# Row weights by small transfers instead of 4-row products, with a reordered first stage and router

## The chip, the cores and the metric

The kernel runs on one core of a Trainium2 chip. The metric is the device time of one execution in microseconds (us), lower is better. Times of the profile are those of one profiled execution; engines are named as the profile names them: PE (matrix multiplies, PEld its weight loads), DVE (VectorE), ACT (ScalarE), POOL (GpSimd), SP (SyncE, which only issues DMAs).

## What is computed

One inference step of a one-layer encoder trunk on 336 tokens: 64 of a sample stream, 16 learned meta tokens and 256 prompt tokens, model width 1024, all float32. The parts that matter here, cut from the reference:

```
z = rmsnorm(x, g_mix) @ w_in            # first stage, then the projections
qk = silu(causal_conv(qk_pre)); ig, lf = gates of 4 heads from z
# mLSTM, per chunk of 64 tokens (one of 16), 4 heads
inter = b + m;  m_t = max(inter, max(d))
w_intra = exp(d - m_t);  w_inter = exp(inter - m_t)
s = (q @ k.T) * w_intra
num = s @ v + w_inter * (q @ C)
h = num / max(|qn|, exp(-m_t));  C_new = w_prev * C + (w_k * k).T @ v
# latent attention beside it: o_v ("ov"), both merged by gates and w_out
x = x + mixed @ w_out
x2 = rmsnorm(x, g_ffn)
logits = x2 @ w_router + b_router       # top 4 of 32 experts, softmax gates
x = x + sum over the 4 of gate * (swiglu(x2 @ w_gu[e] + b_gu[e]) @ w_dn[e] + b_dn[e])
y = rmsnorm(x, g_final)
```

`w_inter` is one number per head and token. In the kernel a head's weights are a row of 336 numbers on one partition, while the queries that they scale lie with their features on 128 partitions, so each row must reach all partitions. The same holds for the running maximum, which enters `w_intra`.

## The kernel before

Tokens are handled as three row tiles of 128, 128 and 80 (`ROWS`) where they lie on partitions, and as six chunks (`CHUNKS`) in attention and recurrence. The order of the work on each engine is written out by hand, and `job_list` gives the order in which the eight PSUM banks are used: job n uses bank n mod 8, `begin` waits until the job eight places before has been read out (`take`), `filled` waits for PE's result.

**First stage.** SP issues the loads of x, then the identity matrix, then the weight panels in the order of need. ACT issues eight loads of small vectors (`vec_rows`, `conv_rows`), takes the three sums of squares, then three roots; DVE scales the three tiles (L1446), PE turns them ("xT"), DVE multiplies by the norm's gain on the way out of PSUM (L1436), and the first projection `("cq", 0)` begins. The gates of the recurrence (`igfr`) come next; DVE works them out in rows of 4 partitions after a wait on `ld_mem`, which counts the broadcast of the router's bias too. Then come the low-rank keys (`lat`), which `keys_turned` needs.

**Attention.** Four pairs of heads (`hp`), each with nine steps `c` in which scores, softmax and value products of six chunks are staggered. Between these steps whole projections are put in as cover (`mla_fill`: query/key and value columns, eight 128x336 products each). In the last pair, the steps 5 and 6 have such a cover, and step 7 has the four products "wi".

**Recurrence's row weights.** `wrow` holds two rows for each of 4 heads: `R_MX` (running maximum) and `R_WI` (w_inter). "wi" are four products of a selector of 4 rows x 128 with `R_WI`, one for each head; ACT copies them to `wib` and takes `wprev` (the weight at the end of each chunk) from there. "mx" are four such products onto 64 partitions each with `R_MX` (L807); DVE turns them into `emat` with the causal mask. After these come the turn of `tail` ("convrow"), the last attention value products `values_out(3)` ("ov"), a wait until ACT has copied these, and the keys and values of chunk 0 turned onto tokens (`keys_values_turned(0)`), then the projection `("o", 0)`.

**Router and experts.** For each row tile: output products ("out", two halves of 512 columns), residual (DVE), norm (ACT square and root, DVE `x2`), turn ("x2T"), router ("lg"), top 4 (DVE `choose`). PE counts with `chosen` which expert gets which token; DVE builds the tables (`tab`, `be`), also the gates as a matrix of tokens by experts (`gmat`), which PE turns ("gT"). POOL gathers the first 64 token rows from DRAM (`rows_in`), PE turns them, ACT copies them to `xg`, and the loop over blocks of 64 tokens starts (`gate_up` at L1030 and L1036, `down` at L1056). SP streams the weights of an expert (12 MB) in 12 transfers, each issued when PE has consumed the piece that it overwrites. `keep_going` issues 128x512 products whose result nobody reads.

## Time and profile before

| what | us |
|---|---|
| median of 3 runs | 1691.27 (1687.09 to 1694.07) |
| the profiled execution | 1689.88 |
| its span, first to last instruction | 1688.1 |
| PE busy in the span | 1530.1 |
| DVE busy in the span | 355.5 |
| ACT busy in the span | 349.8 |
| POOL busy in the span | 122.3 |

The stages by the trace: first stage up to 19.16 us (the first projection starts), projections and attention to about 300 us, recurrence, gates and merging to 532 us, output, router and tables to 605.56 us (the first product of an expert), experts and the final norm to the end.
### The profile page before, as it was taken

To read this page: it belongs to the slowest core of one execution; us is meant where nothing else is said; L and a number is where in the kernel's file an instruction comes from. 1 tells how busy PE (TensorE), PEld (TensorE's weight loads), DVE (VectorE), ACT (ScalarE), POOL (GpSimd) and SP (SyncE) were. 2 spreads that over 40 slices of the span, in tenths; PEclk is the share of its full clock that TensorE was granted. 3 is DMA by queue.
4 is the path that set the end of the run, shared out by engine and by line. 5 is a ranking of instruction groups with operands and counts; after the bars stand their busy time and mean duration, and the time that the engine had idled before them with its cause. 6 is when DMAs were issued, how large, how long until landed. Compare 5 with 4: busy or idle time off the path is not lost.

```text
span 1688.1 us, 20518 instructions
## 1 busy us (share of the span) xinstructions
PE 1530.1 (91%) x7108; PEld 698.8 (41%) x7109; DVE 355.5 (21%) x859; ACT 349.8 (21%) x676; POOL 122.3 (7%) x219
## 2 busy tenths in 40 slices
PE   6999999999999999788799988878999887998993
PEld 4666666666665533222233332222333222333331
DVE  3655432243301330101010110100111001011015
ACT  3434423543200201111111110111111111111111
POOL 0100000000000000001001010000010000001010
PEclk9999999999999989899899998989999998999997
DMA  6311222212284359999989899999898999669897
GB/s 234 107 57 71 101 99 76 76 51 100 90 282 165 133 191 401 408 419 417 408 325 408 341 415 416 416 406 422 321 405 355 410 414 405 262 266 414 342 411 271
DMA packets 92393, 477.38 MB, mean 283 GB/s; under 512 B 12995, under 2 KB 16944, under 8 KB 43074
## 3 DMA queue, kind: packets, MB, share of 16 engines
q1 hardware_dynamic: 84312, 461.79, 69.1%
q0 software_dynamic: 7808, 15.00, 2.7%
q8 instruction: 23, 0.38, 0.1%
q10 hardware_dynamic: 234, 0.08, 0.0%
q14 instruction: 16, 0.13, 0.0%
HBM read 471.28 MB, written 15.50 MB: 288 GB/s over the span
## 4 chain that ended last, share of the span: by engine, by line
PE 73%; DMA 18%; DVE 4%; issue 3%; SPq 1%; ACT 1%; DVEq 0%; POOL 0%; ACTq 0%; POOLq 0%
PE bank L611 28%; PE bank L1030 21%; DMA ring<-in_w_gate_up 17%; PE bank L1056 16%; PE bank L615 3%; PE bank L1036 1%; DVE r_kv L1436 1%; DVE r_v L1439 1%; PE bank L878 1%; DVE r_c L1439 1%; DVE r_qk L1433 0%; SPq L565 0%; PE bank L724 0%; SPq L572 0%; PE bank L873 0%
## 5 line engine op out<-in xcount | busy, mean ns | idle before, releaser
L1030 PE MATMUL bank<-ring,r_kv 128*64 128x512 f32 x2184 | 521.1, 624 | 87.1 <-DMA ring<-in_w_gate_up 87.1
L1030 PEld LDWEIGHTS bank<-ring,r_kv 128*64 128x64 f32 x2184 | 157.1, 142 | 398.5 <-issue 305.6
L1056 PE MATMUL bank<-ring,r_kv 128*64 128x512 f32 x1248 | 289.5, 607 | 0.7 <-ACT r_kv L1126 0.7
L611 PE MATMUL bank<-r_xt,ring 128*128 128x336 f32 x848 | 250.9, 451 | 2.6 <-DVE r_xt L1436 2.4
L1433 DVE TENSOR_SCALAR r_kv<-bank 128x512 f32<-128x512 f32 (+1 forms) x80 | 55.0, 687 | 921.6 <-PE bank L1036 916.1
L611 PEld LDWEIGHTS bank<-r_xt,ring 128*128 128x128 f32 x848 | 159.1, 191 | 79.8 <-issue 8.0
L1056 PEld LDWEIGHTS bank<-ring,r_kv 128*64 128x64 f32 x1248 | 92.6, 143 | 196.0 <-issue 195.1
L1126 ACT ACTIVATE r_xt<-bank 128x512 f32<-128x512 f32 x39 | 23.3, 598 | 507.0 <-PE bank L1056 507.0
L1379 ACT ACTIVATE r_o<-r_kv 128x512 f32<-128x512 f32 x39 | 24.6, 632 | 323.7 <-DVE r_kv L1433 323.7
L615 PEld LDWEIGHTS bank<-const,r_v 64*128 64x128 f32 (+3 forms) x524 | 49.7, 157 | 77.5 <-DVE r_v L1439 44.0
L1036 PE MATMUL bank<-ring,r_kv 128*64 128x512 f32 x312 | 73.5, 592 | 0.0
L615 PE MATMUL bank<-const,r_v 64*128 64x64 f32 (+3 forms) x524 | 64.0, 258 | 10.4 <-DVE r_v L1439 10.4
L611 PE MATMUL bank<-ring 128*128 128x336 f32 (+2 forms) x288 | 70.6, 434 | 0.0
L1126 ACT ACTIVATE r_kv<-bank 128x512 f32<-128x512 f32 (+3 forms) x85 | 49.8, 586 | 82.2 <-PE bank L615 76.9
L611 PE MATMUL bank<-ring,r_kv 128*128 128x128 f32 (+4 forms) x192 | 59.1, 444 | 1.2 <-DVE r_kv L1436 1.2
L611 PEld LDWEIGHTS bank<-ring 128*128 128x128 f32 (+2 forms) x288 | 45.9, 192 | 21.4 <-issue 3.9
L1379 ACT ACT_TABLE_LOAD x39 | 50.0, 1283 | 12.8 <-ACT r_xt L1126 12.6
L1020 PE MATMUL bank<-bgu,r_qk 32*64 32x512 f32 x312 | 43.3, 624 | 8.8 <-DVE r_kv L1433 8.8
L1949 POOL COPY r_qk<-r_qk 128x1 uint32 x39 | 7.9, 202 | 554.8 <-ACT r_xt L1126 554.8
L1953 POOL DMA_INDIRECT y_rows<-r_xt,r_qk x39 | 41.1, 1053 | 34.4 <-POOL r_qk L1949 34.4
L1925 POOL DMA_INDIRECT r_v<-x_rows,r_qk x41 | 39.4, 961 | 54.6 <-POOL r_qk L1942 33.1
L611 PEld LDWEIGHTS bank<-ring,r_kv 128*128 128x128 f32 (+3 forms) x192 | 30.3, 182 | 28.8 <-issue 23.2
(248 smaller groups left out, 945.8 us busy)
## 6 DMA issues: line engine op xcount, KB each, us to landing
ring<-in_w_gate_up SPq DMA_DIRECT2D x256, 1024.0 KB, 17.8
ring<-in_w_down SPq DMA_DIRECT2D x128, 1024.0 KB, 14.9
ring<-in_w_in SPq DMA_DIRECT2D x12, 2048.0 KB, 8.2
ring<-in_w_proj_b SPq DMA_DIRECT2D x2, 2048.0 KB, 8.4
ring<-in_w_proj_a SPq DMA_DIRECT2D x2, 2048.0 KB, 9.3
ring<-in_w_out SPq DMA_DIRECT2D x2, 2048.0 KB, 7.9
ring<-y_rows SPq DMA_DIRECT2D x8, 512.0 KB, 8.5
ring<-in_w_uq SPq DMA_DIRECT2D x2, 1152.0 KB, 8.9
```

Source lines behind the costliest of these rows:

```text
L611: ins = pe.matmul(out, l, r, start=(n == 0), stop=(n == len(pairs) - 1), **kw)
L615: return pe.transpose(out, src, ident[0:src.shape[0], 0:src.shape[0]])
L1020: pe.matmul(half(gate_bank if q < 2 else up_bank, q % 2), pick[32 * q:32 * q + 32, :], bgu[32 * q:32 * q + 32, :], start=True, stop=False, ...
L1030: ins = pe.matmul(half(gate_bank if q < 2 else up_bank, q % 2), xg[:, k, :], w[:, 512 * q:512 * q + 512], start=False, stop=False, skip_gr ...
L1036: ins = pe.matmul(half(bank_, t), xg[:, 7, :], w[:, 512 * (q0 + t):512 * (q0 + t) + 512], start=False, stop=True, skip_group_check=True)
L1056: ins = pe.matmul(half(out_bank, t), hidT[:, 2 * (j % 2) + s, BLK * h:BLK * h + BLK], w[:, s, 512 * t:512 * t + 512], start=(j == 0 and s ...
L1126: return act.activation(out, src, ACT.Copy, scale=scale)
L1379: act.activation(sg, gt, ACT.Sigmoid, scale=ALPHA).then_inc(m_sig, 1)
L1433: return dve.tensor_scalar(out, a, s1, s2, op0, op1)
L1439: return dve.scalar_tensor_tensor(out=out, in0=a, scalar=s, in1=b, op0=op0, op1=op1)
L1925: pool.indirect_dma_start(xrow, None, x_rows_dram[:, :], bass.IndirectOffsetOnAxis(ap=column[0:BLK, :].bitcast(U32), axis=0), bounds_check ...
L1953: pool.indirect_dma_start(y_rows_dram[:, :], bass.IndirectOffsetOnAxis(ap=now[:, 1:2].bitcast(U32), axis=0), yrow, None, bounds_check=8 * ...
```

## The change

It has three parts, and a fourth that follows from them.

1. **First stage.** The identity is loaded by ACT's queue ahead of everything else; one more small vector (the gain of the second norm) is loaded. ACT does a root on a dummy value first, and then square and root of tile 0 before the squares of tiles 1 and 2. DVE scales each tile as soon as its root is there, and the way out of PSUM is shared: ACT does the second half of tiles 0 and 1 (eight copies of 128x128), DVE the other four. PE issues 20, 4, 4 and 7 products of 128x128 whose result nobody reads (`warm`) around the turns. ACT squares both `ckv` before it does the gates' exponentials.
2. **Row weights.** POOL writes `wrow` to DRAM (into rows of `y_rows`) when the gates are done, waits for that, and loads it back broadcast: the maxima onto twice 64 partitions (`emat`), the weights of heads 2 and 3 onto 128 (`wib_hi`), and later, when the convolutions no longer use `u_pad`, those of heads 0 and 1 into `u_pad`. POOL takes `wprev` from there; DVE applies the mask at the start of the second pair of heads. The eight products, ACT's twelve copies and the selector are gone. In the last pair of heads, the projections that stood in steps 5 and 6 stand in 6 and 7. `values_out(3)` stands behind `keys_values_turned(0)`.
3. **Router.** PE turns the residual x1 half by half as soon as it is there, rather than the normed x2; the norm's gain is multiplied into the router's weights, and its scale is applied to the logits. x2 is still made for the gather.
4. **Gates.** The normalised gates, `gmat` and its turn move behind the tables and into the first expert's products; the bias products of the first block move ahead of the turn of the gathered rows.

The core of the diff:

```diff
 def mla_fill(hp, at):
 
+    if hp == 3:
+        at = {5: None, 6: 5, 7: 6}.get(at, at)
     n = 6 * hp + FILL_AT[at] if at in FILL_AT else len(FILL_MLA)
...
+            def warm(b, n):
+
+                for _ in range(n):
+                    pe.matmul(b[:, 0:128], ident, ident, start=True, stop=True, skip_group_check=True)
+
             pe.wait_ge(ld_ident, 16)
...
+            warm(begin("convT"), 20)
             for t, (c0, n) in enumerate(ROWS):
+                if t == 1:
+                    pe.wait_ge(ld_vec, 128)
+                    b = begin("vecT")
+                    end(turn(b[:, 0:NVEC], vec_rows[0:NVEC, :]), "vecT")
+                    warm(begin("convT"), 4)
+                if t == 2:
+                    warm(begin("convT"), 4)
                 pe.wait_ge(xn_ready, t + 1)
...
+            pe.wait_ge(ld_conv, 16)
+            b = begin("convT")
+            end(turn(b[:, 0:48], conv_rows[:, :]), "convT")
+            warm(begin("cq", 0), 7)
...
-                    if hp == 3 and c == 7:
-                        for h in range(4):
-                            b = begin("wi", h)
-                            end(group(b[:, 0:NT], [(cst("sel", 4)[:, 128 * h:128 * h + 128], R_WI)]), "wi", h)
-            for p in range(2):
-                b = begin("mx", p)
-                for g in range(2):
-                    h = p + 2 * g
-                    ins = pe.matmul(b[64 * g:64 * g + 64, 0:NT], cst("sel", 4)[:, 128 * h:128 * h + 64], R_MX, start=True,
-                                    stop=True, skip_group_check=True)
-                end(ins, "mx", p)
...
-            values_out(3)
...
             keys_values_turned(0)
+            values_out(3)
+            for hp in range(4):
+                for h in (0, 1):
+                    taken(pe, "ov", hp, h)
...
             out_half(0, 0)
             out_half(0, 1)
...
+            out_half(1, 0)
+            x1_turned(0, 0)
+            x1_turned(0, 1)
+            out_half(1, 1)
+            pe.wait_ge(w_rt_set, 1)
+            router(0)
+            out_half(2, 0)
+            x1_turned(1, 0)
+            x1_turned(1, 1)
+            out_half(2, 1)
+            x1_turned(2, 0)
+            router(1)
+            x1_turned(2, 1)
...
             count(0)
-            keep_going(begin("x2T", 2, 0), 2)
-            x2_turned(2)
             router(2)
...
+            def gates_turned():
+
+                pe.wait_ge(gates_set, 1)
+                for t, (c0, m) in enumerate(ROWS):
+                    ins = turn(xt_bank[0:NE, c0:c0 + m], gmat[0:m, t, :])
+                ins.then_inc(gT_full, 1)
+
             pe.wait_ge(ld_bgu, 64)
             bias(0)
+            nb = pe.value_load(nbi[0:1, 0:1].bitcast(I32), min_val=NE, max_val=MAXB)
+            pe.wait_ge(m_xrow, 16)
+            tokens_turned()
             pe.wait_ge(m_xg, 1)
             for k in range(8):
+                if k == 1:
+                    gates_turned()
...
+            pool.wait_ge(gates4, 1)
+            pool.dma_start(y_rows_dram[0:8, 0:NT].rearrange("(q h) t -> h q t", q=2), wrow[:, :, :]).then_inc(gates_out, 16)
+            pool.wait_ge(gates_out, 16)
+            for g in range(2):
+                pool.dma_start(emat[64 * g:64 * g + 64, :, :],
+                               y_rows_dram[2 * g:2 * g + 2, 0:NT].unsqueeze(0).broadcast_to([64, 2, NT])).then_inc(mx_in, 16)
+            pool.dma_start(wib_hi[:, :, :], y_rows_dram[6:8, 0:NT].unsqueeze(0).broadcast_to([128, 2, NT])).then_inc(wi_in, 16)
...
+            pool.wait_ge(tail_done, 16)
+            pool.wait_ge(qk_ready, 16)
+            pool.dma_start(u_pad[:, :, 0:NT], y_rows_dram[4:6, 0:NT].unsqueeze(0).broadcast_to([128, 2, NT])
+                           ).then_inc(wi_in, 16)
+            pool.wait_ge(wi_in, 32)
+            for h in range(4):
+                pool.tensor_copy(wprev[:, h, 0:1], wib(h)[:, 63:64])
+                ins = pool.tensor_copy(wprev[:, h, 1:6], wib(h)[:, 79:NT:64])
+            ins.then_inc(wprev_ready, 1)
...
             for hp in range(4):
+                if hp == 1:
+                    dve.wait_ge(mx_in, 32)
+                    for p in range(2):
+                        signal(stt(emat[:, p, :], emat[:, p, :], -1.0, cst("mask"), ALU.mult, ALU.add), emat_set, p + 1)
```

PE at its start, before: `vec_rows` and `conv_rows` are turned first, then the tiles of x (in `ring`), then the first projection.

```order
L615 MATMUL bank<-const,vec_rows 128x109
L615 MATMUL bank<-const,conv_rows 128x48
L615 MATMUL bank<-const,ring 128x128 x16
L615 MATMUL bank<-const,ring 128x80 x8
L611 MATMUL bank<-r_xt,ring 128x336 x8
```

The same place now:

```order
L620 MATMUL bank<-const 128x128 x20
L615 MATMUL bank<-const,ring 128x128 x8
L615 MATMUL bank<-const,vec_rows 128x117
L620 MATMUL bank<-const 128x128 x4
L615 MATMUL bank<-const,ring 128x128 x8
L620 MATMUL bank<-const 128x128 x4
L615 MATMUL bank<-const,ring 128x80 x8
L615 MATMUL bank<-const,conv_rows 128x48
L620 MATMUL bank<-const 128x128 x7
L611 MATMUL bank<-r_xt,ring 128x336 x8
```

Products on the identity (L620) stand between the turns, and the small vectors come after tile 0.

PE from step 6 of the last pair of heads to the first projection of the recurrence, before (`r_xt` with `ring` is a projection that serves as cover, `wrow` the row weights, `tail` the convolution's state; `ring` alone is "ov"):

```order
L611 MATMUL bank<-r_xt,ring 128x336 x8
L611 MATMUL bank<-ring,r_kv 128x128 x4
L615 MATMUL bank<-const,r_c 128x128 x2
L615 MATMUL bank<-const,r_c 16x128
L611 MATMUL bank<-wrow,const 128x336 x4
L611 MATMUL bank<-r_c,r_kv 128x128 x6
L807 MATMUL bank<-wrow,const 64x336 x4
L615 MATMUL bank<-const,tail 96x128
L611 MATMUL bank<-ring 128x336 x4
L615 MATMUL bank<-const,r_qk 64x128 x8
L615 MATMUL bank<-const,r_v 64x128 x8
L848 MATMUL bank<-r_qk 64x64 x8
```

Now:

```order
L611 MATMUL bank<-r_xt,ring 128x336 x8
L611 MATMUL bank<-ring,r_kv 128x128 x4
L615 MATMUL bank<-const,r_c 128x128 x2
L615 MATMUL bank<-const,r_c 16x128
L611 MATMUL bank<-r_xt,ring 128x336 x8
L611 MATMUL bank<-r_c,r_kv 128x128 x6
L615 MATMUL bank<-const,tail 96x128
L615 MATMUL bank<-const,r_qk 64x128 x8
L615 MATMUL bank<-const,r_v 64x128 x8
L844 MATMUL bank<-r_qk 64x64 x8
L611 MATMUL bank<-ring 128x336 x4
```

A projection stands where "wi" stood, "mx" is gone, and "ov" has moved behind the turned keys and values.

PE at the end of the tables, before (`r_o`,`r_kv` is "tab", `r_qk` with `const` is "be" and then "gT", `r_v` the gathered rows, `bgu` the experts' bias, `ring` with `r_kv` the first expert's products):

```order
L980 MATMUL bank<-r_o,r_kv 64x55 x24
L611 MATMUL bank<-r_qk,const 128x55
L615 MATMUL bank<-const,r_qk 32x128 x2
L615 MATMUL bank<-const,r_qk 32x80
L1008 TENSOR_LOAD r_qk
L1008 ISA x2
L962 MATMUL bank<-const 128x512
L615 MATMUL bank<-const,r_v 128x64 x8
L1020 MATMUL bank<-bgu,r_qk 64x512 x4
L1030 MATMUL bank<-ring,r_kv 64x512 x8
```

Now:

```order
L986 MATMUL bank<-r_o,r_kv 64x55 x24
L611 MATMUL bank<-r_qk,const 128x55
L914 MATMUL bank<-const 128x512 x2
L1018 MATMUL bank<-bgu,r_qk 64x512 x4
L1068 TENSOR_LOAD r_qk
L1068 ISA x2
L615 MATMUL bank<-const,r_v 128x64 x8
L1028 MATMUL bank<-ring,r_kv 64x512 x4
L615 MATMUL bank<-const,r_qk 32x128 x2
L615 MATMUL bank<-const,r_qk 32x80
L1028 MATMUL bank<-ring,r_kv 64x512 x4
```

The bias products stand ahead of the gathered rows, and "gT" behind the first piece of the first expert.

## Rows read from the trace of the kernel before

**Rows 1.** The page: span, and the chain that ended last, by engine

```profile
span 1688.1 us, 20518 instructions
...
PE 73%; DMA 18%; DVE 4%; issue 3%; SPq 1%; ACT 1%; DVEq 0%; POOL 0%; ACTq 0%; POOLq 0%
```

**Rows 2.** Windows (busy us, granted clock, DMA share, GB/s), and PE's waits in the experts

```profile
640.00:660.00 20.00, 19.54 (x102) 6.96 (x100) 2.83 (x5) 3.71 (x5) 2.58 (x4) 1.00 1.01 414
...
PE bank L1030 <- DMA ring<-in_w_gate_up: 87.1, 17, 7.1
```

**Rows 3.** Timeline of the first stage: start, us, engine, line, what, idle before

```profile
6.44 1.06 ACT L1140 ACTIVATE ring<-ring 128x1024 f32<-128x1024 f32 x1 [0.89 <-DMA ring<-in_x_prompt]
...
10.34 1.28 ACT L1144 ACT_TABLE_LOAD   x1
...
12.13 0.76 DVE L1433 TENSOR_SCALAR ring<-ring,ss 128x1024 f32<-128x1024 f32 x1
...
14.88 3.92 DVE L1436 TENSOR_TENSOR r_xt<-bank,vec 128x512 f32<-128x512 f32 x6
...
19.16 6.43 PE L611 MATMUL bank<-r_xt,ring 128*128 128x336 f32 x16 [2.36 <-DVE r_xt L1436]
```

**Rows 4.** Timeline of the gates and the low-rank keys (DVE, PE)

```profile
30.01 0.06 DVE L1458 MEMSET mst<- 4x1 f32 x1 [11.21 <-DMA b_router_b<-in_b_router]
...
59.95 2.25 DVE L1500 RECIPROCAL r_kv<-r_kv 128x336 f32<-128x336 f32 x1
...
63.71 2.19 PE L615 MATMUL bank<-const,r_kv 128*128 128x128 f32 x12
```

**Rows 5.** Timeline of the last pair of heads: the cover of step 5, and ACT

```profile
274.53 4.68 PE L611 MATMUL bank<-r_xt,ring 128*128 128x336 f32 x16
...
275.26 0.58 ACT L1126 ACTIVATE ring<-bank 128x128 f32<-128x128 f32 x2
```

**Rows 6.** Timeline of PE from step 7 of the last pair to the recurrence

```profile
285.41 1.05 PE L611 MATMUL bank<-ring,r_kv 128*128 128x128 f32 x8
...
286.72 2.85 PE L611 MATMUL bank<-wrow,const 4*128 4x336 f32 x8
...
293.25 2.50 PE L807 MATMUL bank<-wrow,const 4*64 4x336 f32 x8
...
295.92 3.97 PE L611 MATMUL bank<-ring 128*128 128x336 f32 x8
300.69 1.04 PE L615 MATMUL bank<-const,r_qk 128*64 128x128 f32 x8 [0.80 <-ACT r_o L1126]
...
303.14 1.11 PE L611 MATMUL bank<-r_xt,ring 128*128 128x336 f32 x3
```

**Rows 7.** Windows with the granted clock (last but two), first projection and 4-row products

```profile
20.00:24.00 4.00, 4.00 (x11) 2.50 (x10) 0.00 (x0) 0.00 (x0) 0.00 (x0) 0.68 1.08 370
290.00:294.00 4.00, 4.00 (x16) 2.77 (x17) 0.54 (x2) 1.29 (x6) 0.00 (x0) 0.50 0.68 253
```

**Rows 8.** Timeline of the router of tiles 1 and 2 (PE)

```profile
576.82 1.87 PE L611 MATMUL bank<-r_xt,r_o 128*128 128x32 f32 x16
...
582.82 1.30 PE L611 MATMUL bank<-r_xt,r_o 128*80 128x32 f32 x16 [0.82 <-ACT r_o L1126]
```

**Rows 9.** Timeline from the table product to the first expert

```profile
594.90 1.61 PE L980 MATMUL bank<-r_o,r_kv 128*64 128x55 f32 x48
...
597.37 0.27 DVE L1433 TENSOR_SCALAR r_qk<-bank,const 64x55 f32<-64x55 f32 x1
...
602.61 1.11 PE L615 MATMUL bank<-const,r_v 64*128 64x64 f32 x8
...
603.76 0.60 ACT L1126 ACTIVATE r_kv<-bank 128x512 f32<-128x512 f32 x1 [5.95 <-PE bank L615]
...
605.56 0.96 PE L1030 MATMUL bank<-ring,r_kv 128*64 128x512 f32 x2
```

**Rows 10.** Timeline: DVE's last work in the first pair of heads

```profile
111.37 0.62 DVE L1604 COPY ring<-bank 128x128 f32<-128x128 f32 x2 [1.26 <-PE bank L611]
```

More of the change, by code:

```diff
@@ L162, in job_list @@
                 j += [mla_fill(hp, n)]
-            if hp == 3 and n == 7:
-                j += [("wi", h) for h in range(4)]
-    j += [("mx", p) for p in range(2)] + [("convrow",)] + [("ov", 3, h) for h in (0, 1)]
+    j += [("convrow",)]
     def turned(c):
         return [("krow", c, s) for s in range(2)] + [("vrow", c, s) for s in range(2)] + [("s", c)] if c < 6 else []
-    j += turned(0)
+    j += turned(0) + [("ov", 3, h) for h in (0, 1)]
     for c in range(6):
@@ L816, in _ @@
             pe.wait_ge(qk_ready, 16)
-            for hp in range(4):
-                for h in (0, 1):
-                    taken(pe, "ov", hp, h)
             def heads_turned(c):
@@ L909, in _, with keep_going @@
             pe.wait_ge(mix_a, 16)
+            def keep_going(b, n):
+                for _ in range(n):
+                    pe.matmul(b[:, :], ident, const[:, 0:512], start=True, stop=True, skip_group_check=True)
             def out_half(t, s):
@@ L915, in out_half, with x1_turned @@
                 end(group(b[0:m, :], [(mixed[:, k, c0:c0 + m], PV[f"wo{s}"][:, k, :]) for k in range(8)]), "out", t, s)
-            def x2_turned(t):
+            def x1_turned(t, s):
                 m = ROWS[t][1]
-                pe.wait_ge(x2_ready, t + 1)
-                for s in range(2):
-                    b = begin("x2T", t, s)
-                    for k in range(4):
-                        ins = turn(b[:, m * k:m * k + m], x2[0:m, t, 128 * (4 * s + k):128 * (4 * s + k) + 128])
-                    end(ins, "x2T", t, s)
+                taken(pe, "out", t, s)
+                b = begin("x1T", t, s)
+                for k in range(4):
+                    ins = turn(b[:, m * k:m * k + m], x1[0:m, t, 128 * (4 * s + k):128 * (4 * s + k) + 128])
+                end(ins, "x1T", t, s)
             def router(t):
@@ L985, in _ @@
             end(group(b[:, 0:NB1], [(cst("ones")[0:NE, :], cmpT[:, :])]), "be")
-            pe.wait_ge(gates_set, 1)
-            b = begin("gT")
-            for t, (c0, m) in enumerate(ROWS):
-                ins = turn(b[0:NE, c0:c0 + m], gmat[0:m, t, :])
-            end(ins, "gT")
-            taken(pe, "gT")
             def down_bias(b, t, s):
@@ L1160, in _ @@
                 take(copy(cq[:, n, :], bank(("cq", n))[:, 0:NT], vec[:, V_GQ + n:V_GQ + n + 1]), "cq", n)
+            for n in range(2):
+                filled(act, "ckv", n)
+                signal(act.activation(sq[:, 3 + n, :], bank(("ckv", n))[:, 0:NT], ACT.Square), cq_ready, n + 4)
+            for n in range(2):
+                take(copy(lat[:, n, :], bank(("ckv", n))[:, 0:NT]), "ckv", n)
             act.wait_ge(gates_x, 1)
@@ L1164, in _ @@
             signal(act.activation(R_WK, R_WK, ACT.Exp), gates4, 1)
-            for n in range(2):
-                filled(act, "ckv", n)
-                signal(act.activation(sq[:, 3 + n, :], bank(("ckv", n))[:, 0:NT], ACT.Square), cq_ready, n + 4)
-                take(copy(lat[:, n, :], bank(("ckv", n))[:, 0:NT]), "ckv", n)
             for t in range(4):
@@ L1613, in _ @@
             signal(dve.tensor_copy(C[:, :, 256], vec[:, V_N0:V_N0 + 8]), n_set, 1)
-            for p in range(2):
-                filled(dve, "mx", p)
-                take(stt(emat[:, p, :], bank(("mx", p))[:, 0:NT], -1.0, cst("mask"), ALU.mult, ALU.add),
-                     "mx", p)
             def heads_out(c):
@@ L1806, in _ @@
             signal(dve.tensor_copy(idx[:, 1, :].bitcast(U32), idxf[:, 1, :]), idx_set, 2)
+            for t in range(3):
+                dve.wait_ge(gate_e, t + 1)
+            step(dve.reciprocal(gsum[:, 0:3], gsum[:, 0:3]))
+            step(tt(gate[:, :, 0:4], gate[:, :, 0:4], gsum[:, 0:3].unsqueeze(2).broadcast_to([128, 3, 4]), ALU.mult))
+            step(tt(prod, onehot, gate[:, :, 0:4].unsqueeze(3).broadcast_to([128, 3, 4, NE]), ALU.mult))
+            signal(dve.tensor_reduce(gmat, prod.rearrange("p t k e -> p t e k"), AX.X, ALU.add), gates_set, 1)
             for n in range(6):
```

207 lines of the change are left out of this document (116 added, 91 removed).

## Prediction, made before the changed kernel was run

> **What bounds the kernel now.** I read the page first: its chain of what ended last is 73% PE and 18% DMA, in a span of 1688.1 us [rows 1]. So nearly everything that PE does in order, and nearly every wait of PE, is paid in full until the experts start at 605.56 [rows 9]. From there on two engines share the bound: in a window of the expert loop the DMA share is 1.01 at 414 GB/s, and PE waits 87.1 us for weights in 17 waits, yet in this same window it is busy 19.54 of 20 us [rows 2]. The transfers of expert 1 are issued as PE consumes expert 0, so the loop as a whole hangs on the moment at which the first expert's products begin. What is won before that moment should move the end by as much. Then I read the timeline at the three places that the change touches, and windows for the granted clock there.
>
> What to see in them. In the first stage, the roots come after all three squares and a table load, so the first tile is scaled only at 12.13, the turned tiles leave PSUM by one engine in six operations (3.92 us), and the first projection starts at 19.16 and takes 6.43 us for 16 passes [rows 3]; at full clock 16 such passes take 4.68 [rows 5]. The granted clock there is 0.68 [rows 7]. In the recurrence's head, PE is busy 4.00 of 4.00 us and the clock is 0.50, that is 1.2 GHz [rows 7]: everything from the 4-row products at 286.72 to the turned keys at 300.69 [rows 6] goes at half speed without PE having paused. At the router, PE waits for what DVE and ACT do between the last output product and the last router product [rows 8], later for DVE and the gather [rows 9].
>
> **First stage.** Square 0 begins at 6.44 and takes 1.06 [rows 3]. With the root right behind it (a dummy root has loaded the table before, so the 1.28 us load of 10.34 is off the path [rows 3]) I put the scaling of tile 0 at 8.8 instead of 12.13. The last tile gains less: two squares and a root lie ahead of its root, and DVE has tile 1, one way out of PSUM and the scaling of 0.76 ahead of it. I put its scaling at 13.2 to 14.1, its turn at 15.0, the last two ways out (0.5 each, of the 3.92 for six) at 16.0. The seven `warm` products, 14 passes of 128 columns at 0.13 (1.05 for eight, [rows 6]), stand in PE's order and end near 16.8. So the projection starts 2.35 us earlier. As PE is given products from some 6 us on, I take it at full clock: 6.43 - 4.68 = 1.75. Together **4.1**. Bounds: if the 20 products start late and run at half clock they end near 15.5 and the turns queue behind them, which leaves about 0.5; without the seven in the way it is 5.6. Does a later wait eat it? DVE's gate chain cannot start before the router's bias has landed at 30.01 [rows 4], and it hardly moves (SP issues one load less and a smaller constant). Its followers are ready for PE's turn of the keys when the keys' scaling ends at 59.95, and PE comes at 63.71 [rows 4]: 3.7 us of slack against 4.1 of gain, 0.4 exposed at worst, and ACT's earlier squares of `ckv` pull that chain forward too. I charge nothing.
>
> **Row weights.** From the first "wi" at 286.72 to the projection at 303.14 before: 16.4 us [rows 6]. In the same stretch now: the last attention product, 12 passes at 0.13 = 1.6; the turned tail 0.2; keys and values 303.14 - 300.69 = 2.45 [rows 6]; "ov" 8 passes at 4.68/16 = 0.29 [rows 5], 2.3, instead of the 3.97 in rows 6; and the wait for ACT, 0.80, which stays: ACT now has two exponentials, four scaled copies and two more copies ahead of the two "ov" copies, and by their durations is just done with them when the second "ov" product ends. Sum 7.35, saved 9.1. Against it: the cover of step 5 of the last pair has moved to step 7. PE then reaches at 274.53 what ACT has ready at 275.26 + 0.58 [rows 5], a hole of 1.4. Net **7.7**. High bound 9.1 (no hole), low bound 3.4: only the columns of the products go, eight passes at 0.29 and the 2.50 of L807 [rows 6], less the hole, and the clock still falls. I take the high clock, since the fall begins with these products and PE never idled. The transfers themselves lie on POOL, idle then until the key rows are stored after 64 us; DVE's masks (1.0) and POOL's copies have a 4.7 us projection as cover. If the cover goes, they cost these same microseconds.
>
> On the clock the Trainium skill (TensorE: Matmul & The Clock Gate, "What's actually happening") says that the gate follows how busy PE has recently been, and names idleness as what lowers it. The window with 4.00 of 4.00 busy at 0.50 does not agree with idleness as the only cause. By that rule alone the fall would have another cause and could stay, which gives the low bound above.
>
> **Router and tables.** Before, from the end of router 1 (576.82 + 1.87) to router 2 (582.82) 4.13 us pass, with the last wait of 0.82 on ACT [rows 8]. Now there are four turns ahead of router 1 and four behind it (0.4 each), the count (0.6) and one filler of 0.95, the copies being hidden: 2.35. Gain 1.8. Making x2 for tile 2 (1.3) moves on DVE behind the choice, beside PE's last count of the same length; I charge 0. Next, the table product ends at 596.51, but DVE, delayed by the gates' two large operations, reads it at 597.37 [rows 9]: 0.86 gained, not the full 1.4, because then PE's product is late. Next, the gathered rows are turned at 602.61 and are in `xg` at 604.36, but the first product starts at 605.56, because the bias products stand between [rows 9]; they move ahead: 1.1. The turn of the gates now costs 0.4 inside the first expert. Net **3.3**; bounds 1.5 (x2 and its store delay the gather, clock lower) to 5.
>
> **Sum.** 4.1 + 7.7 + 3.3 = 15.1. The profiled execution is 1689.88, 1.8 more than its span, so it becomes 1674.8. The median of the runs is 1.4 above the profiled one. I forecast **1675.5**, 0.9% faster. The low bounds add up to 5.4 of gain, the high ones to 19.7.
>
> **Rivals.**
> A, the forecast: the gains reach the end, 1671 to 1680.
> B, the change doesn't do what it seems to for the clock: 3.4 instead of 7.7 in the recurrence. For it: the stretch has short waits and small products besides. Against it: the clock is at half exactly there. 1680.
> C, the fillers of the first stage stand in the way: PE starts its projection hardly earlier and only the clock's 1.75 is won. 1678.
> D, the gain is given back in the experts. Their 1080 us hold 17 waits for weights, PE's clock falls in some, and the three runs differ by 7 us. If phases shift against each other there by 1%, up to 10 us go: 1686.
> E, slower: DVE stands at the head of the second pair of heads for the broadcast maxima. The price is one for one, since all queries of that pair wait behind it. DVE gets there at 112, by row 111.37 [rows 10], less 4. The transfers start at about 52, so there are 56 us of room. The nearest row is a broadcast of 128 short rows, for which DVE sat 11.21 us [rows 4], under 0.1 us a row with the queues full. The 256 rows here are ten times as long; at 0.1 each they need 26. It becomes slower than before by 0.5% once they need 56 + 15 + 8 = 79, or 0.3 a row; at 0.4 they need 102 and the kernel 1722. Against it: they are spread over the engines in a stage with a low DMA load.
>
> The Trainium skill (DMA: Bandwidth & Descriptors, "Anatomy of one DMA") gives about 2.0 us fixed and little more for such a transfer issued by POOL. By an estimate from that page all of them are in by 60 us, and rival E would not exist. No row of before shows such a transfer.
>
> **Chances.** A 0.62, B 0.12, C 0.11, D 0.12, E 0.03. Half a percent, 8.5 us, is about what a measurement of this kernel can tell from no change; the bound is 1682.8. A, B and C lie below it, D mostly not: faster 0.85, same 0.12, slower 0.03. The range reaches from the high bounds and a fast run (1667) to B and C together with a slow run (1683).
>
> **What would show it.** Right: first projection near 16.8 with 16 passes in 4.7; clock 1.00 from the last attention step to the first chunk; a PE wait of about 1.4 on ACT in step 6 of the last pair; from there to the "o" projection 7 to 8 us; DVE reading the table the moment PE has made it; the first expert's product near 590.5; the loop after it as long as before. Wrong: a clock of 0.50 again before the recurrence; a new PE wait between 40 and 65 us on the gates or keys; DVE idle at the head of the second pair; the first expert 15 us earlier but the end not.

## The result and the profile after

The changed kernel takes 1682.14 us (median of 6 runs, 1677.66 to 1688.45), against 1694.63 for the kernel before in runs of the same session (1687.09 to 1696.56). The ratio is 0.994, with a 95% interval of 0.9922 to 0.9958. A second session gave 0.9936 (0.9913 to 0.996). So the change wins some 10.5 us, 0.6%. I had forecast 0.9%, with a lower end at 0.5%: the direction is right and a third of the gain is missing. The profiled execution is the longest of its six, 1688.45, and only 1.5 us shorter in its span than that of before. It shows where this one execution lost its gain, not what the median lost.

The page of the changed kernel: span, granted clock in 40 slices of 42 us, and the chain that ended last. Below them, PE's waits for weights in the experts (us, times, longest).

```profile
span 1686.6 us, 20635 instructions
...
PEclk9979999999999999898899999889999998999996
...
PE 73%; DMA 17%; DVE 4%; issue 3%; SPq 1%; ACT 1%; ACTq 0%; DVEq 0%; POOL 0%; POOLq 0%
...
PE bank L1028 <- DMA ring<-in_w_gate_up: 89.4, 17, 7.0
```

The bound is what it was in [rows 1]. The third slice of the clock, 84 to 126 us, has a 7.

**First stage.** Timeline of the changed kernel; columns as in [rows 3]:

```profile
2.75 7.07 PE L620 MATMUL bank<-const 128*128 128x128 f32 x40 [2.75 <-DMA const<-in_consts]
...
9.09 0.75 DVE L1471 TENSOR_SCALAR ring<-ring,ss 128x1024 f32<-128x1024 f32 x1
...
16.82 4.69 PE L611 MATMUL bank<-r_xt,ring 128*128 128x336 f32 x16
...
59.62 2.19 PE L615 MATMUL bank<-const,r_kv 128*128 128x128 f32 x12
```

The first tile is scaled at 9.09 instead of 12.13, and the projection starts at 16.82 and takes 4.69 where it took 6.43 from 19.16 on [rows 3]: 4.1 us by 21.5. The keys are turned at 59.62 and not at 63.71 [rows 4], so the 4.1 us are still there and no wait on DVE took their place.

**First pair of heads.** Timeline of PE from the first turned probabilities on, of the changed kernel:

```profile
85.35 0.77 PE L615 MATMUL bank<-const,ring 128*128 128x128 f32 x5 [1.01 <-DVE ring L1471]
...
87.58 2.07 PE L611 MATMUL bank<-ring,r_c 128*128 128x128 f32 x8
...
93.18 2.74 PE L611 MATMUL bank<-r_kv,ring 128*128 128x208 f32 x6
...
101.66 5.48 PE L611 MATMUL bank<-r_xt,ring 128*128 128x336 f32 x16
...
108.82 3.56 PE L611 MATMUL bank<-r_xt,ring 128*128 128x336 f32 x12
```

and the same products in the kernel before, which I had not looked at closely:

```profile
89.44 0.76 PE L615 MATMUL bank<-const,ring 128*128 128x128 f32 x5 [1.02 <-DVE ring L1433]
...
91.65 1.13 PE L611 MATMUL bank<-ring,r_c 128*128 128x128 f32 x8 [0.51 <-ACT ring L1126]
...
94.75 1.52 PE L611 MATMUL bank<-r_kv,ring 128*128 128x208 f32 x6
...
99.33 4.68 PE L611 MATMUL bank<-r_xt,ring 128*128 128x336 f32 x16
...
105.69 4.69 PE L611 MATMUL bank<-r_xt,ring 128*128 128x336 f32 x16
```

Windows of four us of the changed kernel, then one of the kernel before (stretch, PE, PEld, DVE, ACT, POOL busy, granted clock, DMA share, GB/s):

```profile
84.00:88.00 4.00, 2.99 (x15) 2.28 (x16) 2.15 (x10) 3.21 (x8) 0.31 (x2) 0.77 0.97 323
88.00:92.00 4.00, 4.00 (x18) 3.55 (x17) 0.65 (x4) 0.47 (x2) 0.00 (x0) 0.50 0.53 201
...
100.00:104.00 4.00, 4.00 (x13) 2.88 (x13) 3.29 (x10) 1.12 (x4) 0.00 (x0) 0.59 0.00 0
```

```profile
92.00:96.00 4.00, 4.00 (x26) 3.17 (x25) 0.81 (x3) 0.48 (x3) 0.00 (x0) 1.00 0.53 200
```

The instructions and the first wait (1.0 us on DVE) are the same. But within a microsecond of that wait's end the changed kernel's clock falls to 0.50, that is 1.2 GHz, for some 17 us (worked out from the windows), and PE, busy without a pause, runs its small products at half speed. From 85.35 to 108.82 are 23.5 us; from 89.44 to 105.69 were 16.2. So 7.2 us go here, more than the first stage had won. In the kernel before a second wait of 0.51 follows 1.7 us after the first; in this profile of the changed kernel the products at half speed fill it.

**Last pair of heads and the recurrence.** PE in the changed kernel from the hole of step 6 to the output projection:

```profile
279.01 1.73 PE L611 MATMUL bank<-ring,r_kv 128*128 128x128 f32 x8 [1.19 <-ACT ring L1137]
...
281.11 6.20 PE L611 MATMUL bank<-r_xt,ring 128*128 128x336 f32 x16
...
292.90 2.08 PE L611 MATMUL bank<-r_c,r_kv 128*128 128x128 f32 x12
294.90 0.31 PE L615 MATMUL bank<-const,tail 128*96 128x128 f32 x1
295.06 1.04 PE L615 MATMUL bank<-const,r_qk 128*64 128x128 f32 x8
...
297.51 2.53 PE L611 MATMUL bank<-ring 128*128 128x336 f32 x8
```

```profile
290.00:300.00 10.00, 10.00 (x64) 7.20 (x62) 2.22 (x8) 4.84 (x11) 0.00 (x0) 1.00 0.59 205
```

The head of the recurrence runs at full clock (1.00, where [rows 7] had 0.50): the two "ov" products take 2.53 instead of the 3.97 of [rows 6], and the output projection starts at 300.94, behind the wait of 0.90 on ACT. That stretch is 8.0 us long and not 16.4. But the hole costs more than its own length: the projection behind it takes 6.20 where it takes 4.69 at full clock [rows 5].

**Router and tables.**

```profile
575.12 1.91 PE L611 MATMUL bank<-r_xt,r_o 128*128 128x32 f32 x16
...
578.90 1.27 PE L611 MATMUL bank<-r_xt,r_o 128*80 128x32 f32 x16
...
591.19 1.61 PE L986 MATMUL bank<-r_o,r_kv 128*64 128x55 f32 x48 [0.81 <-DVE r_kv L1474]
...
592.92 0.27 DVE L1471 TENSOR_SCALAR r_qk<-bank,const 64x55 f32<-64x55 f32 x1 [0.75 <-PE bank L986]
...
599.19 3.68 PE L1028 MATMUL bank<-ring,r_kv 128*64 128x512 f32 x8 [0.69 <-ACT r_kv L1137]
```

From the router of tile 1 to that of tile 2 there are 3.8 us and not 6.0 [rows 8]. DVE now waits for the table product, not the other way round. The first expert starts at 599.19 instead of 605.56 [rows 9]. From the output projection of the recurrence to there it is 298.2 us instead of 302.4.

The ledger of the profiled execution, as differences to before: first stage −4.1; first pair of heads +7.2; hole +1.6 and slow projection +1.5; head of the recurrence −8.4; router and tables −4.2; from the first expert's product to the end 1087.4 instead of 1082.5, +4.9. Sum −1.5.

### The profile page after: what moved, and what is told of

Read it like the earlier page. It is cut to its first block, busy times and chain, and to the rows that moved or that the text cites. A ratio compares the mean times of both kernels' runs of the same rounds, so it can differ in the third digit from the quotient of the medians.

```text
span 1686.6 us, 20635 instructions
## 1 busy us (share of the span) xinstructions
PE 1539.3 (91%) x7162; PEld 708.3 (42%) x7163; DVE 354.9 (21%) x859; ACT 348.3 (21%) x672; POOL 126.1 (7%) x232
## 4 chain that ended last, share of the span: by engine, by line
PE 73%; DMA 17%; DVE 4%; issue 3%; ACT 1%; SPq 1%; ACTq 0%; DVEq 0%; POOL 0%; POOLq 0%
PE bank L611 28%; PE bank L1028 21%; DMA ring<-in_w_gate_up 17%; PE bank L1054 17%; PE bank L615 3%; PE bank L1034 1%; DVE r_kv L1474 1%; DVE r_v L1477 1%; PE bank L878 1%; DVE r_c L1477 1%; SPq L565 0%; PE bank L735 0%; DVE r_qk L1471 0%; SPq L572 0%; PE bank L873 0%
## 5 line engine op out<-in xcount | busy, mean ns | idle before, releaser
L615 PE MATMUL bank<-const,r_v 64*128 64x64 f32 (+3 forms) x524 | 63.7, 257 | 11.6 <-DVE r_v L1477 10.3
L611 PE MATMUL bank<-r_kv,ring 128*128 128x336 f32 (+9 forms) x192 | 44.7, 362 | 0.0
```

Of the source, the lines that this page charges most:

```text
L611: ins = pe.matmul(out, l, r, start=(n == 0), stop=(n == len(pairs) - 1), **kw)
L615: return pe.transpose(out, src, ident[0:src.shape[0], 0:src.shape[0]])
```

## Experiments

**Each part alone.** Three kernels are the kernel before with one part of the change: the first stage (squares, roots, scaling, throw-away products `warm`), the row weights (transfers, masks, cover moved), the router with the tables. The fourth is the whole change with throw-away products in three pauses of PE:

```
 turn_probs:  + if (hp, c) == (0, 0): warm(begin("pT", 0, 0, 0), 7)
                pe.wait_ge(pnorm, u + 1)
 attend:      + b = begin("ol", hp, c)
              + if (hp, c) in ((0, 0), (3, 3)): warm(b, 4 if hp == 0 else 8)
                taken(pe, "pT", hp, c, p)
```

> The kernel before with the change's first stage alone. Theory S (shift): the first projection starts near 16.8 as in the whole change, everything up to the first pair of heads lies 4.1 us earlier, and that alone makes PE's granted clock fall at 86 to 103 us: small products of the first pair at half speed, 7 us lost, time 0.1% to 0.2% above the kernel before. Rival R (the row transfers, which share the queues at 50 to 90 us, or what POOL and DVE do for them): no fall here, clock 1.00 in all of 80 to 110 us, and 4.1 us faster (0.9976). Rival E (it falls in some executions of any version): the profile may show either, and the median lies between.

Measured 0.9982 (0.9963 to 1.0002). The profile: the clock falls at the same place, without any row transfer in the kernel. Theory S is right on that, rival R falls.

```profile
85.03 0.77 PE L614 MATMUL bank<-const,ring 128*128 128x128 f32 x5 [1.01 <-DVE ring L1467]
...
87.25 2.05 PE L610 MATMUL bank<-ring,r_c 128*128 128x128 f32 x8 [0.52 <-ACT ring L1136]
```

But the time is not above that of before. Seven of its 12 runs lie at 1686.1 to 1687.9 and five at 1691.5 to 1696.2, with mean clocks of 0.948 to 0.951 and 0.944 to 0.948; the profiled one is in the upper group. So such a fall may come in a part of the executions only, which is rival E of this expectation.

> The kernel before with the row weights by transfers alone. Theory S: the first pair of heads stays where it was and at full clock; a hole of 1.2 to 1.4 us in step 6 of the last pair; head of the recurrence at full clock, 8 us instead of 16.4 from the last attention product to the output projection: 6 to 8 us faster (0.9955). Rival R: the clock falls at 88 to 105 us, 7 us lost there, so that the whole is about as before (0.9995).

Measured 0.9964 (0.9949 to 0.998). No fall in the first pair of heads. Here the hole of 1.20 us stays without a slow projection behind it, and the head goes as in the whole change:

```profile
276.12 1.73 PE L612 MATMUL bank<-ring,r_kv 128*128 128x128 f32 x8 [1.20 <-ACT ring L1116]
...
278.06 4.69 PE L612 MATMUL bank<-r_xt,ring 128*128 128x336 f32 x16
...
296.37 0.80 PE L612 MATMUL bank<-r_xt,ring 128*128 128x336 f32 x2 [0.90 <-ACT r_o L1116]
```

The projection starts 6.8 us before that of [rows 6]. With the 4-row products gone, 290 to 300 is at 1.00. That they alone were what the half clock hung on is not shown: the same edit puts a projection where "wi" stood and moves "ov" behind the turned keys.

> The kernel before with the router and the tables alone. From the o projection to the first expert's product 4.2 us less, and nothing changed before 560 us. If the expert loop keeps it: 0.9975. If the loop gives gains back by a shifted phase of its weights and clock: between 0.998 and 1.001, with the first expert's product 4 us earlier in its profile all the same.

Measured 0.998 (0.9963 to 0.9997). The first expert's product came at 601.18, 4.4 us earlier; from there to the end 1087.3 us.

The three parts add up to 0.74%, 12.5 us.

> The whole change, and throw-away products of 128 columns in three places where PE waits: 7 before the first turned probabilities of the first pair of heads (the wait of 1.0 us at 85.35), 4 before its first attend product, 8 before the attend product of step 6 in the last pair (the hole of 1.19 us). Nothing else is changed, and each fits into its wait. Theory S with the pauses as the trigger: the clock stays at 1.00 in 84 to 104 and 280 to 288, 7 to 9 us less than the whole change (0.989 of the kernel before). If the fall doesn't come from these pauses: no gain, 0.994 as the whole change, clock 0.5 again at 88 to 100.

Measured 0.9939 (0.9917 to 0.9961), with a profile of 1677.97 us, clock 1.00 in every window from 80 to 120 and from 280 to 300. That is a first sign that the fall hangs on the pauses, but the times were not better: I had taken a `warm` for one pass, and it is two. The 7, 4 and 8 took 1.7, 1.0 and 1.8 us in pauses of 1.0, 0.5 and 1.2, some 1.7 too many in all. That is 0.1%, and the 0.989 expected lies 0.5% lower, outside the interval: the 7 to 9 us of the one profile were not there to be won in the others.

**Trimmed covers, and a shift in time.** The second set has the changed kernel again, the covers cut to 4, 2 and 5, and the changed kernel delayed by 8 or 16 more throw-away products ahead of the first projection (`warm(begin("cq", 0), 7)` with 15 or 23 in place of 7).

> The changed kernel itself once more, on the chip of the three others. If its clock falls in the first pair of heads in every execution, this profile shows 0.50 there again and the executions lie within some 6 us; if only in some executions, the profile may show 1.00, and the times spread over 7 us more with the mean clock (0.948 with, 0.955 without). Median 1682 either way.

Measured 0.9936 (0.9913 to 0.996). The profile has the fall again at the same place (0.50 from 88 to 104), and the six runs go from 1675.63 to 1691.57, with mean clocks of 0.955 down to 0.945: a spread that a fall in only some of them could make.

> The changed kernel with throw-away products cut to the length of the three waits (4, 2 and 5 instead of 7, 4 and 8, which had overshot by 1.7 us). If the pauses trigger the fall, as the covers run showed in one profile: clock 1.00 in 84 to 104 and 280 to 288, first expert's product near 591, 1.7 us less than covers and 8 less than the changed kernel's profile with the fall. If the fall needs less than that to come back, it is back here.

Measured 0.9911 (0.9894 to 0.9928), 1677.27 us (1674.0 to 1680.73), the fastest of all, beside 1683.45 for the changed kernel on the same chip. The covers end where the waits ended:

```profile
84.04 1.16 PE L620 MATMUL bank<-const 128*128 128x128 f32 x8
85.12 0.77 PE L615 MATMUL bank<-const,ring 128*128 128x128 f32 x5
...
86.75 0.71 PE L620 MATMUL bank<-const 128*128 128x128 f32 x4
87.38 1.13 PE L611 MATMUL bank<-ring,r_c 128*128 128x128 f32 x8
```

```profile
88.00:92.00 4.00, 4.00 (x25) 2.98 (x23) 0.58 (x2) 0.19 (x1) 0.00 (x0) 1.00 0.47 174
```

Its first expert starts at 590.30, where I had forecast 590.5 for the change itself, and its 0.89% is 15 us. That does not bring the forecast back: this kernel has three covers that the kernel before lacks, and two of them make that kernel faster too (the control below).

> The changed kernel with 16 more throw-away products (32 passes, 4.2 us at 0.131 each) right before its first projection, so that all that follows lies where it did in the kernel before, with PE as busy from the start as in the changed kernel. Theory P (the place in time decides): no fall at 84 to 104 us, the 7.2 us there come back, the recurrence's head and the router gain as in the changed kernel: 3 us faster than the changed kernel in spite of 4.2 us more work (0.992 of the kernel before). Theory H (what PE did in the first 80 us decides: it is at full clock and full load from 3 us on): the fall stays, 4 us slower than the changed kernel (0.9965).

Measured 0.9958 (0.9939 to 0.9977). The fall stays, at the same instruction, now at 88.5:

```profile
88.52 0.76 PE L615 MATMUL bank<-const,ring 128*128 128x128 f32 x5 [1.02 <-DVE ring L1471]
...
90.73 2.04 PE L611 MATMUL bank<-ring,r_c 128*128 128x128 f32 x8 [0.51 <-ACT ring L1137]
```

By the expectation that speaks for theory H. But eight of the 11 runs lie at 1680 to 1687 and three at 1693 to 1695, so here too only a part seems to fall.

> The same with 8 more (2.1 us). Theory P: the fall is there or not, by the place alone, and if it is there it starts nearer to the same time (86 to 88 us) than to the same instruction. Theory H: the fall starts 2.1 us later than in the changed kernel, at the same instruction, and the time is 2 us above the changed kernel.

Measured 0.9942 (0.9924 to 0.996). The fall starts at the same instruction (87.0) but is short: 0.92 in 84 to 88, 0.65 in 88 to 92 and 1.00 from 92 on make 3.4 us of half clock. So its length varies as well as its coming. Neither theory had that.

**What in the first stage does it, and does the kernel before fall too?**

> The changed kernel without the throw-away products of its first stage (20, 4, 4 and 7), so that PE is idle there between its turns as in the kernel before, while the order of squares, roots, scalings and ways out stays. Theory H (PE busy and at full clock from 3 us on is what makes the clock fall at 86 us): full or part fall gone, clock 1.00 in 84 to 104; the first projection starts at 15 to 15.5 but at lower clock, so at 21 us it is about as early as in the changed kernel; time 1678 to 1680 (0.992). Rival (the fall hangs on something else of the first stage, such as the order of the gates' exponentials behind the squares of the latents): the fall is there at the same instruction, 1683 or slower.

Measured 0.9944 (0.9925 to 0.9963). The fall is there, 0.50 from 92 to 104, with PE idle in the first stage up to 9.60. Theory H falls: the throw-away products are not needed for it. The first turned probabilities stand at 87.32 here and at 85.35 with the throw-away products.

> The kernel before with throw-away products in the two pauses of its first stage alone (7 before the first turn of x, 8 before the first projection). Nothing moves but the clock. Theory H: 1.00 instead of 0.68 in 20 to 24, the projection in 4.7 instead of 6.4, and the clock falls at 88 us at the first turned probabilities, in some or all executions: time 0.998 to 1.003 of the kernel before, spread in two groups 7 us apart. Rival: only the 1.7 us are won (0.999) and the clock stays at 1.00 in 84 to 104.

Measured 1.0005 (0.9988 to 1.0022). The projection took 4.76, as expected, and there is no fall at 94 to 108, against theory H again. Instead PE met a wait that the kernel before doesn't show:

```profile
52.69 3.92 PE L611 MATMUL bank<-r_v,const 128*128 128x336 f32 x6 [2.33 <-ACT r_v L1173]
```

It waits for the squares of the latents, which stand behind the gates' exponentials on ACT. PE came here 1.2 us earlier, and the gates later, because DVE had got the router's bias later than in [rows 4]:

```profile
31.72 0.06 DVE L1464 MEMSET mst<- 4x1 f32 x1 [12.43 <-DMA b_router_b<-in_b_router]
```

The clock was then 0.55 to 0.60 up to 60 us. The control below, the kernel before with covers in the first pair of heads, has the same wait, shorter, and its clock stays at 1.00 there:

```profile
51.95 2.10 PE L611 MATMUL bank<-r_v,const 128*128 128x336 f32 x6 [0.89 <-ACT r_v L1175]
```

So the kernel before has a second place of the same sort. It is open in two of the six profiles with the first stage of before, those in which the bias came latest (at 31.72 and 30.99, against 29.6 to 30.1 in the others). None of the profiles with the changed first stage shows this wait; it has the squares ahead of the exponentials. In this one profile the place cost more than the full clock of the first stage had won; the ratio of the runs shows neither a gain nor a loss.

> The changed kernel with only the two covers of the first pair of heads (4 and 2 throw-away products). If the fall there is what the median lost: 0.9925 of the kernel before or less, no fall at 84 to 104; the hole in step 6 of the last pair stays (1.19 us) and with it the projection of 6.2 to 6.4 us behind it at part clock, 1.5 us. If the hole's share was the larger: 0.994 as the changed kernel.

Measured 0.9915 (0.9893 to 0.9938), 1679.52 us. That is 0.2% to 0.25% below the changed kernel, so these two pauses cost its runs some 4 us, though the intervals overlap. The hole of step 6 stays, with a projection of 6.74 behind it:

```profile
274.91 6.74 PE L611 MATMUL bank<-r_xt,ring 128*128 128x336 f32 x16
```

With the hole covered too, in the kernel of the trimmed covers, it takes 4.69:

```profile
273.68 4.69 PE L611 MATMUL bank<-r_xt,ring 128*128 128x336 f32 x16
```

Of the eight profiles that have the hole uncovered, six show 6.2 to 6.95 for this projection and two show 4.69; the three with a cover show 4.69. The ratios of the two kernels (0.9915 and 0.9911) can't tell these 2 us.

> Control: the kernel before with the same two covers. If the fall in the first pair of heads belongs to the change, nothing is to be had here: 1.000, within 0.2%. If the kernel before falls there too in some executions, which its one profile missed: 0.998 or less.

Measured 0.9985 (0.9971 to 0.9999), its 12 runs from 1688.76 to 1694.08 where the 29 of the kernel before beside them go from 1687.98 to 1700.78. So the kernel before loses here too in some executions, about 2.5 us on average, which its one profile did not show. The interval touches 0.9999, so this is likely and not certain.

This control and the changed kernel with the same two covers ran on one chip and differ by the change alone. Their runs have means of 1691.1 and 1679.5 us: with the two pauses filled in both kernels the change is worth 11.6 us (by my estimate from their scatter, 9 to 14). It is worth 10.5 without covers. So the falls in the first pair of heads take about 1 us more from the changed kernel than from the kernel before, and they are not the whole of the missing third.

**Place or chance.** The last set: the changed kernel delayed by 24 more throw-away products (31 in place of 7), the kernel before again, and the trimmed covers without the throw-away products of the first stage.

> The changed kernel with 24 more throw-away products before its first projection (6.3 us), so that the first turned probabilities come at 90 to 91 us, behind the 89.4 of the kernel before. Theory P (the place in time decides, with a bound between the 88.5 of the 4 us delay, which fell, and the 89.4 of before, which didn't): clock 1.00 in 84 to 108 and executions in one group; 1681 to 1684 in spite of 6.3 us more work. Theory N (it may fall at this instruction in any execution, by chance, and the first stage raises or doesn't raise the share): the fall is in this profile or not, and the executions lie in two groups; median 1687 to 1690.

Measured 0.9964 (0.994 to 0.9988), 1689.52 us. The profile has no fall:

```profile
90.86 0.76 PE L615 MATMUL bank<-const,ring 128*128 128x128 f32 x5 [1.02 <-DVE ring L1471]
...
93.07 1.13 PE L611 MATMUL bank<-ring,r_c 128*128 128x128 f32 x8 [0.51 <-ACT ring L1137]
```

That is what theory P expected of the clock. The median is above its 1681 to 1684. The 12 runs, from 1676.64 to 1696.07 with mean clocks of 0.957 to 0.947, and this median are what theory N expected.

> The kernel before once more. Theory N: its executions fall too, in a part of them (the control with covers had the upper end of the times cut off, 1694 instead of 1701); this profile shows either clock 1.00 or 0.50 at 90 to 105 us. Theory P: 1.00 again. Ratio 1.000.

Measured 0.9988 (0.9969 to 1.0007), which is also the noise of such a comparison. No fall in the first pair of heads at 89.23. But the head of the recurrence took from 286.52 to 301.17, 14.7 us instead of the 16.4 of [rows 6]: the fall there comes earlier or later within this stretch too.

> The changed kernel with the three trimmed covers (4, 2 and 5) and without the throw-away products of its first stage. If the fall was all that those products risked or cost, and they buy the 1.9 us by which the projection ends earlier: 1.5 to 2 us slower than covers_trim2, 0.992 of the kernel before. No fall in 84 to 108, since the pauses are filled. If the clock before 80 us mattered for the fall, it is back.

Measured 0.9911 (0.9884 to 0.9938), 1680.82 us: no fall, and no loss against the trimmed covers that these intervals could tell. The profiles do show one: the first turned probabilities stand at 87.91 and not at 85.12, and the first expert starts at 593.06 and not at 590.30. So the throw-away products buy 2.8 us there, and the new order of squares, roots and scaling the other 1.5 from the 89.44 of before.

## Why the prediction was off

**First stage: the size was right, the charge of nothing was not.** "So the projection starts 2.35 us earlier" and the 1.75 of the clock came out to a tenth (16.82, 4.69). The check of what is late next looked for waits on other engines and found none, rightly. The step that failed is "I charge nothing": I took PE's stretch between 85 and 110 to keep its 16.2 us. It holds pauses of 1.0 and 0.5 us among small products, and with the first stage moved it took 23.5 us in the profile. All six profiles with the changed first stage, no cover and less than 6 us of delay have the fall there, and the four with covers have none, so the pauses are its cause; which of the two it hangs on was not separated, since the covers fill both. Over all runs the charge is smaller than in the profile, because not every execution seems to fall and the kernel before loses some too: the first stage alone was worth 3.0 us (0.9982) and not 4.1, with an interval that holds both, and the comparison with covers in both kernels gives about 1 us as well.

How often the fall comes, and how it depends on the place, is open. In the profiles without a cover, the clock fell there where the first turned probabilities stood at 85.03, 85.11, 85.35, 87.01, 87.32 or 88.52, and did not at 89.23, 89.40, 89.44, 89.67, 90.86 or 93.95. Twelve profiles agree with a bound by place near 89. But all six that fell have the changed first stage, and of the six that didn't only that of the 6 us delay has it, so one profile carries the bound. The times don't agree with it: those of the 6 us delay spread as widely as any. The Trainium skill (TensorE: Matmul & The Clock Gate, "What's actually happening") says that the window in which the clock gate looks at PE is free-running and doesn't reset when a kernel starts. By that rule the same pause may matter in one execution and not in the next, which the spread of the times agrees with and the twelve profiles neither need nor exclude.

**Row weights: right in mechanism, a little too large.** Forecast 7.7, measured alone 0.9964, 6.1 us (3.4 to 8.6). The clock holds, as I chose against rival B, and the stretch is 8.0 us for my 7.35. Two things are missing. The 7.35 was too short: the last attention products took 2.0 for my 1.6, "ov" 2.5 for 2.3 and the wait 0.9 for 0.8. And the 9.1 was taken against one execution's 16.4, where the six profiles with 4-row products have 14.7 to 17.7, mean 16.1: the saving is 8.0 on average. The hole was 1.6 for my 1.4. That the projection behind it might go slower was not priced: 1.5 us in this profile, none in the part alone, and 1.5 us or more in six of the eight profiles with the hole open. Here too I had charged a pause of PE with its length only.

**Router and tables: right.** Forecast 3.3, measured alone 0.998, 3.4 us (0.5 to 6.3). In the profile 4.2 by the first expert. From the output projection of the recurrence to the first expert's product it is 301.8 to 302.4 us in the six profiles without the router part and 298.0 to 300.5 in the eleven with it, 3.1 less on average. The five slowest of the eleven have 10 to 14 us of half clock between 570 us and the first expert, the others 3 to 7; what makes that difference was not tested.

**Rival D, the experts.** The profile gives back 4.9 us there, at most 3.2 of it in one wait for weights:

```profile
1429.61 2.83 PE L1028 MATMUL bank<-ring,r_kv 128*64 128x512 f32 x6 [6.98 <-DMA ring<-in_w_gate_up]
```

which was 3.79 in the kernel before:

```profile
1432.99 3.68 PE L1030 MATMUL bank<-ring,r_kv 128*64 128x512 f32 x8 [3.79 <-DMA ring<-in_w_gate_up]
```

Over all profiles the time from the first expert's product to the end is 1082.3 to 1086.0, mean 1083.8, in the six without the router part, and 1081.4 to 1089.3, mean 1085.5, in the eleven with it. The two overlap, and the three parts alone sum to 12.5 us where the whole is 10.5, within their intervals. A give-back of some 2 us is possible and not shown.

**Rivals B and C fell, and E too.** B falls with the clock of 1.00 in the recurrence's head, C with the projection at 16.82. The transfers of the maxima were issued at 54.0 and took 3.1 us to land, and DVE makes the masks at 121.9 without waiting for them. That is later than the 112 less 4 of the prediction: the copy at 111.37 [rows 10] was not DVE's last of the first pair of heads, which stands at 118.13 in the kernel before. So the room was larger than I took it for. The estimate from the Trainium skill (DMA: Bandwidth & Descriptors, "Anatomy of one DMA"), all of them in by 60 us, agrees for the three transfers that POOL issues then, though they took 3.1 and 3.9 us, more than 2.0 "and little more". The fourth, for heads 0 and 1, is issued only at 225.9, when `u_pad` is free.

**The width and what stays open.** The sum took a single profile of before as the kernel, at all three places where the clock matters. The runs of that kernel that I had spread by 7 us, those of the later sets by 9 to 14, and I named that spread under rival D without asking what makes it. The forecast of 1675.5 is also 0.7 below its own sum, since 1691.27 less 15.1 is 1676.2. The ends of my range came from the terms of the change alone. Of the 4.6 us that are missing, by the parts alone 1.1 belong to the first stage and 1.6 to the row weights, each with an interval that holds its forecast as well. The other 2 are open: they too lie within the intervals, and falls of the clock in the router or a give-back in the experts could make them.

## What to carry to other kernels

When a change moves PE's work in time, look at every short pause of PE further on, not only at what is late next: a 1 us wait among small products went with a loss of 7 us to the half clock in one profile, of 1 us in another and of none in a third. Fill such a pause with throw-away products into a bank that is begun anyway, as long as the wait and no longer: what overshoots is paid (1.7 us here). Give the kernel before the same fillers, or their gain is taken for that of the change. Take the spread of the times of a kernel as a hint of such places, and don't size a term from the clock that a single profile shows.

## What the hardware showed

- The granted clock fell to 0.50 for 3.4 to 17 us (worked out from the windows) behind waits of 1.0 and 0.5 us among small products, while PE was busy again without a pause (windows at 4.00 of 4.00 busy and 0.50), in six of six profiles with the first turned probabilities at 85.0 to 88.5 us and no cover; in none of the four with covers there.
- The same behind the hole of 1.2 us in the last pair of heads: the projection behind it took 6.2 to 6.95 instead of 4.69 us in six of eight profiles, and 4.69 in all three with a cover.
- Products of 4 rows go with a clock of 0.50 in all six profiles that have them, with 14.7 to 17.7 us for a stretch that takes 8.0 to 8.2 in the new order without them.
- Filling the two pauses of the first pair of heads narrows the runs of a kernel: 5 to 8 us from lowest to highest in the five kernels with covers (6 or 12 runs each), 9 to 19 in most without. The row weights alone (6.3 in 12 runs) and the 2 us delay (7.3 in 6) are as narrow without one, and few runs spread less than many, so the spread isn't proof by itself.
- A transfer of 2 rows to each of 128 partitions (336 KB written) landed 3.9 us after issue in the changed kernel, and cost POOL 0.75 us.
